# A hybrid streaming encoder layer on one core: the borders between recurrence, attention, merge and projections rearranged

## What is computed

```python
h = rmsnorm(x, norm_mix_g)
qkv, z, b_raw, a_raw, dq, dk, dv, gate_a, gate_b = split(h @ w_in)
o_a = gated_delta_rule(...)                    # branch A: 8 heads, chunks of 64 frames
o_a = rmsnorm(o_a, norm_g) * silu(z)
s = q k^T * 64 ** -0.5 - slope * dist          # branch B: two maps for each of 8 heads
p = softmax(s)
o_b = rmsnorm((p[0] - lam * p[1]) @ v) * (1 - lam_init)
x = x + (sigmoid(gate_a) * (o_a @ w_branch_a) + sigmoid(gate_b) * (o_b @ w_branch_b)) @ w_out
x = x + cross_attend(rmsnorm(x), mem_k, mem_v, w_mq, w_mo)     # 4 heads, 256 memory tokens
x = x + peer(rmsnorm(x))                       # 128*128 one-neuron experts
return rmsnorm(x)
```

## Time and profile before

| | us |
|---|---|
| median of 3 runs | 5154.19 |
| lowest and highest | 5153.65 to 5163.55 |
| the profiled execution | 5151.6 |
| its span, first to last instruction | 5150.0 |
| TensorE busy in it | 4952.7 |
| VectorE busy | 3119.4 |
| ScalarE busy | 1607.4 |

### The profile page before, as it was taken

One profiled execution on the slowest core, in us unless ns is written; L12 is line 12 of the kernel. 1 busy time (PEld: TensorE's weight loads), 2 busy tenths in 40 slices (PEclk: granted clock), 3 DMA queues, 4 the chain that ended last, 5 costly groups with the idle time before them and its releaser, 6 DMA issues.

```text
span 5150.0 us, 83445 instructions
## 1 busy us (share of the span) xinstructions
PE 4952.7 (96%) x35997; PEld 4795.7 (93%) x35997; DVE 3119.4 (61%) x3919; ACT 1607.4 (31%) x1776; POOL 744.1 (14%) x606
## 2 busy tenths in 40 slices
PE   8999999998999999999989999999999999999998
PEld 6999988887888899998989999999999999999998
DVE  5355544444445433322279988887676477777777
ACT  4444422223334321213132234443222222222222
POOL 0100000000000000000000022323443122222221
PEclk9999999999999999999999999999999999999999
DMA  6422232222332432231232268888998789999985
GB/s 229 163 103 101 97 94 83 78 86 103 104 103 95 151 122 85 83 114 64 84 131 99 104 241 332 328 324 328 337 345 327 275 328 337 333 335 329 330 327 210
DMA packets 262923, 1010.01 MB, mean 196 GB/s; under 512 B 47744, under 2 KB 127744, under 8 KB 176640
## 3 DMA queue, kind: packets, MB, share of 16 engines
q1 hardware_dynamic: 177696, 547.93, 30.4%
q0 software_dynamic: 68832, 442.58, 22.5%
q10 hardware_dynamic: 16128, 15.60, 0.9%
HBM read 918.77 MB, written 87.24 MB: 195 GB/s over the span
## 4 chain that ended last, share of the span: by engine, by line
PE 75%; DVE 11%; DMA 7%; issue 3%; ACT 2%; DVEq 2%; ACTq 0%; POOL 0%; SPq 0%; POOLq 0%; PEldq 0%
PE psum L1300 20%; PE psum L1112 11%; PE psum L1222 11%; PE psum L918 10%; PE psum L890 7%; PE psum L1129 4%; DMA tmp<-in_u,eidx 2%; DMA arena<-in_u,tiu 2%; PE psum L866 2%; DVE e_lo L2066 2%; PE psum L1268 2%; PE psum L851 2%; DMA arena<-in_u,eidx 1%; DVE arena L2231 1%; DVE tmp L2231 1%
## 5 line engine op out<-in xcount | busy, mean ns | idle before, releaser
L2066 DVE TENSOR_TENSOR e_lo<-ring,e_hi 128x2048 fp32r<-128x2048 f32 x270 | 618.7, 2291 | 284.7 <-ACT e_hi L1551 271.0
L1551 ACT ACTIVATE e_hi<-ring 128x2048 fp32r<-128x2048 f32 x270 | 517.7, 1917 | 811.3 <-PE psum L1300 659.6
L1222 PE MATMUL psum<-h_hi,e_hi 128*128 128x384 f32 x2032 | 698.0, 343 | 34.8 <-DVE e_lo L2066 34.2
L1300 PE MATMUL psum<-c_hi,e_hi 128*128 128x384 f32 x2048 | 686.8, 335 | 13.6 <-DVE H L2311 9.2
L1222 PE MATMUL psum<-h_hi,e_lo 128*128 128x384 f32 x2048 | 690.5, 337 | 0.0
L1222 PE MATMUL psum<-h_lo,e_hi 128*128 128x384 f32 x2032 | 687.1, 338 | 0.0
L1300 PE MATMUL psum<-c_lo,e_hi 128*128 128x384 f32 x2048 | 685.4, 335 | 0.0
L1300 PE MATMUL psum<-c_hi,e_lo 128*128 128x384 f32 x2048 | 685.3, 335 | 0.0
L918 PE MATMUL psum<-p_hi,e_lo 128*128 128x272 f32 x1792 | 519.4, 290 | 0.0
L1222 PEld LDWEIGHTS psum<-h_hi,e_hi 128*128 128x128 f32 x2032 | 383.8, 189 | 42.2 <-issue 19.1
L1300 PEld LDWEIGHTS psum<-c_hi,e_hi 128*128 128x128 f32 x2048 | 385.3, 188 | 18.8 <-DVE e_lo L2066 9.4
(11 more groups left out here) (461 smaller groups left out, 10461.3 us busy)
## 6 DMA issues: line engine op xcount, KB each, us to landing
ring<-in_weights SPq DMA_DIRECT2D x200, 1024.0 KB, 4.8
ring<-in_uT SPq DMA_DIRECT2D x128, 1024.0 KB, 5.4
ring<-in_v SPq DMA_DIRECT2D x128, 1024.0 KB, 9.0
hid<-tmp POOLq DMA_DIRECT2D x128, 192.0 KB, 5.9
gates<-arena POOLq DMA_DIRECT2D x12, 2048.0 KB, 10.1
arena<-hid SPq DMA_DIRECT2D x32, 768.0 KB, 11.1
arena<-gates SPq DMA_DIRECT2D x32, 768.0 KB, 15.0
gate_in<-tmp ACTq DMA_DIRECT2D x64, 136.0 KB, 3.4
```

What stands on the lines that cost most here:

```text
L1222: mm = nc.tensor.matmul(psum[:, 2 + r % 2, 0:ND], w, h[:, c, 0:ND], start=(c == 0 and i == 0), stop=(c == KD - 1 and i == 2))
L1300: mm = nc.tensor.matmul(psum[:, d, 0:ND], w, c[p // 2][:, 2 * (p % 2) + r, :], start=(first and r == 0 and j == 0), stop=(last and r == 1 ...
L1551: nc.scalar.activation(hi_slot(n, reg), e_raw[n % R], ACT.Copy).then_inc(w_rounded, 1)
L2066: nc.vector.tensor_tensor(e_lo[n % R], e_raw[n % R], as_f32(hi_slot(n, reg)), ALU.subtract)\
```

## The change

- **A tile between recurrence and attention.** TensorE fills a whole tile (32 units) after the last chunk, before it waits for `d_o`; ScalarE serves its first half before its own wait and its second after it. A head has 112 units instead of 116, with "vt" 6 instead of 12, a[0] 18 instead of 14, "obs" 4 instead of 6, and three of aT[3]'s six units placed as "os" in front of step 4's waits.
- **Splits and norms in attention.** `splits_at` places a split after the last step that has at least 8 units left until the tile is wanted; `norm_slot` puts the norm of a head after the first step of the next head that has no split.
- **Rounds later.** A round that falls due in an "a" or "obs" stretch is put off until the copy of the transposed probabilities, or the square root, has been made (`round_later`).
- **Branch A ahead of the last norm.** ScalarE rounds OA in the last head (after step 4's exponentials, copies and squares), VectorE splits it before the last norm; OB's first seven heads are rounded before the last one is done. TensorE no longer waits for `done`. The split of the second merge tile comes after OB's.
- **M's first half earlier.** Heads 0 to 7 of M are rounded once branch A of the last merge tile is through (`oa_used`), and split before that tile's merge. The round and split of the second w_out tile move behind that.
- **Sums and waits one tile later.** The sums of X's squares come after the first w_mq tile, the root after all of X is rounded; the first projection starts before ScalarE has taken the small rows (`ba_free`).
- **Three pieces of the cross-attention's output** are rounded in the last head.
- GpSimd waits for the distances before it loads those of the decode rows, and for `x_tile` instead of `x_done`.

```diff
-ATT_FILL = {"vt": 12, "a": (14, 12, 14, 16, 17), "aT": (8, 4, 3, 6, 4), "obs": 6}
+ATT_FILL = {"vt": 6, "a": (18, 12, 14, 16, 17), "aT": (8, 4, 3, 3, 4), "os": 3, "obs": 4}
...
-GDN_UNITS, ATT_UNITS = F_CHUNK * F_TILE, 116
+GDN_UNITS, ATT_UNITS = F_CHUNK * F_TILE, 112
...
+P_DONE = [ATT_FILL["vt"] + sum(ATT_FILL["a"][0:q + 1]) + sum(ATT_FILL["aT"][0:q]) + (ATT_FILL["os"] if q == 4 else 0)
+          for q in range(QT)]
+SPLIT_UNITS = 8
+def splits_at(h, q):
+    at = ATT_UNITS * h + P_DONE[q]
+    after = ATT_UNITS * (h + 1) + P_DONE[0] if q == QT - 1 else ATT_UNITS * h + P_DONE[q + 1]
+    last = h == HEADS - 1 and q == QT - 1
+    return [k for k in range(2, N_FILL - F_GDN + 1)
+            if F_TILE * (k - 1) >= at + SPLIT_UNITS and (last or F_TILE * (k - 1) < after + SPLIT_UNITS)]
+def norm_slot(h):
+    return next(q for q in range(QT) if not splits_at(h + 1, q)) if h + 1 < HEADS else None
...
             pool.wait_ge(fill_full, 2 * (F_GDN + 1))
+            pool.wait_ge(at["dist_in"], 16)
             pool.dma_start(ndist_s[0:NS, :], t["ndist_s"]).then_inc(at["dist_in"], 16)
...
             mm.then_inc(ba_full, 1)
-            pe.wait_ge(ba_free, 1)
...
                 pe.wait_ge(qk_sq, i * 2 + 2)
+                pe.wait_ge(ba_free, 1)
...
+            u = fill(u, F_TILE)
             pe.wait_ge(s["d_o"], NCH + 1)
...
                     if q == 4:
+                        u = fill(u, ATT_FILL["os"])
                         wait_first(at["cache_in"], h * 32 + 32)
                         wait_first(at["obs"], h * 2 + 1)
...
-            pe.wait_ge(at["done"], HEADS)
...
+                    if d == KD - 1 and k0 == 0:
+                        mm.then_inc(oa_used, 1)
                 mm.then_inc(tile_done, 1)
-            pe.wait_ge(acc_free, freed(T_OUT + 1))
             for d in range(KD):
                 split_tile(T_OUT + d, m_hi, m_lo, S_M)
-            tile_sums(pe, "cross")
             for d in range(KD):
                 split_tile(T_MQ + d, h_hi, h_lo, S_H)
+                if d == 0:
+                    tile_sums(pe, "cross")
...
+            u = serve(u, F_HALF)
             act.wait_ge(s["d_o"], NCH + 1)
             act.wait_ge(outs, 48)
             round_w(T_FILL + F_GDN + 1)
+            u = serve(u, F_HALF)
...
-                    u = serve(u, ATT_FILL["a"][q])
+                    later = []
+                    u = serve(u, ATT_FILL["a"][q], later)
+                    if h == HEADS - 1 and q == 4:
+                        round_branch(oa_hi, OA, 0, 3)
...
+                    round_later(later)
                     u = serve(u, ATT_FILL["aT"][q])
...
-                u = serve(u, ATT_FILL["obs"])
+                u = serve(u, ATT_FILL["obs"], later)
+                if h == HEADS - 1:
+                    round_branch(oa_hi, OA, 6, HEADS)
                 act.wait_ge(at["oss"], h + 1)
                 nc.scalar.activation(ort, aux[0], ACT.Sqrt, bias=eps, scale=1.0 / DH).then_inc(at["rt"], 1)
+                round_later(later)
...
-            act.wait_ge(fill_full, 2 * N_FILL)
+            round_branch(ob_hi, OB, 0, HEADS - 1)
             act.wait_ge(at["done"], HEADS)
-            for k in range(HEADS):
-                round_src(oa_hi, OA, S_OAB, k)
-            for k in range(HEADS):
-                round_src(ob_hi, OB, S_OAB, k)
+            round_branch(ob_hi, OB, HEADS - 1, HEADS)
...
                 if k == 0:
+                    act.wait_ge(oa_used, 1)
+                if k == HEADS:
                     act.wait_ge(tile_done, done(T_OUT - 1))
+                    round_w(W_MERGE + KD + 1)
                 round_src(m_hi, M, S_M, k)
...
                 if k == 1:
                     tile_squares(act, "cross", KD - 1)
-                    tile_root(act, "cross")
+            tile_root(act, "cross")
...
+                else:
+                    for k in range(OC_EARLY):
+                        round_src(m_hi, OC, S_OC, k)
...
-            head_norm(HEADS - 1)
-            split_w(T_MERGE + 1)
...
-            dve.sem_inc(merged, 2)
             for k in range(HEADS):
                 split_src(oa_lo, OA, oa_hi, k, S_OAB)
+            head_norm(HEADS - 1)
+            dve.sem_inc(merged, 2)
             for k in range(HEADS):
                 split_src(ob_lo, OB, ob_hi, k, S_OAB + HEADS)
+            split_w(T_MERGE + 1)
             for d in range(KD):
+                if d == KD - 1:
+                    for k in range(HEADS):
+                        split_src(m_lo, M, m_hi, k, S_M)
```

More of the change, by code:

```diff
@@ L62 @@
             "a_vn": 4, "a_o": 3}
-ATT_FILL = {"vt": 12, "a": (14, 12, 14, 16, 17), "aT": (8, 4, 3, 6, 4), "obs": 6}
+ATT_FILL = {"vt": 6, "a": (18, 12, 14, 16, 17), "aT": (8, 4, 3, 3, 4), "os": 3, "obs": 4}
 F_CHUNK = 3
-GDN_UNITS, ATT_UNITS = F_CHUNK * F_TILE, 116
+GDN_UNITS, ATT_UNITS = F_CHUNK * F_TILE, 112
 assert sum(GDN_FILL[k] for k in ("c_qb", "c_kv", "d_gu", "d_a", "d_rr", "a_vn", "a_o")) \
     + sum(GDN_FILL["d_r"]) + 5 * GDN_FILL["a_x"] == GDN_UNITS
-assert ATT_FILL["vt"] + sum(ATT_FILL["a"]) + sum(ATT_FILL["aT"]) + ATT_FILL["obs"] == ATT_UNITS
-assert GDN_UNITS * (NCH + 1) + ATT_UNITS * HEADS == N_FILL * F_TILE
+assert ATT_FILL["vt"] + sum(ATT_FILL["a"]) + sum(ATT_FILL["aT"]) + ATT_FILL["os"] + ATT_FILL["obs"] == ATT_UNITS
+assert GDN_UNITS * (NCH + 1) + F_TILE + ATT_UNITS * HEADS == N_FILL * F_TILE
 N_WEIGHTS = T_PQ + 16
-UNITS_AT = [ATT_UNITS * h + ATT_FILL["vt"] + sum(ATT_FILL["a"][0:q]) + sum(ATT_FILL["aT"][0:q])
-            for h in range(HEADS) for q in range(QT)] + [ATT_UNITS * HEADS]
+P_DONE = [ATT_FILL["vt"] + sum(ATT_FILL["a"][0:q + 1]) + sum(ATT_FILL["aT"][0:q]) + (ATT_FILL["os"] if q == 4 else 0)
[9 more added lines that the diff above has]
+    return next(q for q in range(QT) if not splits_at(h + 1, q)) if h + 1 < HEADS else None
 W_MERGE = T_MERGE
@@ L767, in _ @@
                 values_of(h)
-            pool.wait_ge(x_done, 2)
+            pool.wait_ge(x_tile, 2 * KD)
             pool.dma_start(t["x_mid"], X).then_inc(x_moved, 16)
@@ L1444, in _, with serve @@
             first_rows(HEADS - 1, True)
-            def serve(u, units):
+            def serve(u, units, later=None):
                 for half in range(u // F_HALF, (u + units) // F_HALF):
@@ L1461, in serve, with round_later @@
                     if b == 1 and n != F_GDN - 1:
-                        round_w(T_FILL + n + 2)
+                        if later is None:
+                            round_w(T_FILL + n + 2)
+                        else:
+                            later.append(T_FILL + n + 2)
                 return u + units
+            def round_later(later):
+                while later:
+                    round_w(later.pop(0))
             def gdn_block(c, dyn, u):
@@ L1504, in _, with round_branch @@
             round_w(T_FILL + F_GDN + 1)
+            u = serve(u, F_HALF)
+            def round_branch(hi, src, first, end):
+                for k in range(first, end):
+                    round_src(hi, src, S_OAB, k)
             for h in range(HEADS):
@@ L1533, in _ @@
                         nc.scalar.activation(osq[:, 0:NP_], ob[:, 0:NP_], ACT.Square)
+                        u = serve(u, ATT_FILL["os"])
+                    if h == HEADS - 1 and q == 4:
+                        round_branch(oa_hi, OA, 3, 6)
                 act.wait_ge(at["o"], h * 5 + 5)
@@ L1608, in _ @@
             act.drain()
-            for k in range(KD):
+            for k in range(OC_EARLY, KD):
                 round_src(m_hi, OC, S_OC, k)
@@ L1924, in _ @@
                 gdn_block(c, slice(c * CH, (c + 1) * CH))
+            split_w(T_FILL + F_GDN + 1)
             dve.wait_ge(at["dist_in"], 16)
@@ L1935, in head_norm @@
                                                in1=ort, op0=ALU.mult, op1=ALU.mult).then_inc(at["done"], 1)
-            def split_tiles(h, q):
-                for k in range(1, N_FILL - F_GDN + 1):
-                    if UNITS_AT[QT * h + q] <= F_TILE * k - 12 < UNITS_AT[QT * h + q + 1]:
-                        split_w(T_FILL + F_GDN + k)
             def attention_head(h):
@@ L1975, in attention_head @@
                                                    op0=ALU.mult, op1=ALU.add).then_inc(at["a"], 1)
-                    if q == 0 and h:
+                    if h and q == norm_slot(h - 1):
                         head_norm(h - 1)
-                    split_tiles(h, q)
+                    for k in splits_at(h, q):
+                        split_w(T_FILL + F_GDN + k)
             for h in range(HEADS):
                 attention_head(h)
-            head_norm(HEADS - 1)
-            split_w(T_MERGE + 1)
             def split_src(lo, src, hi, k, n):
@@ L1988, in split_src @@
                     .then_inc(src_split, 1)
+            for k in range(HEADS):
+                split_src(oa_lo, OA, oa_hi, k, S_OAB)
+            head_norm(HEADS - 1)
             dve.sem_inc(merged, 2)
             for k in range(HEADS):
```

(12 more changed lines are left out.)

9 lines of the change are left out of this document (5 added, 4 removed).

## The result

| | before | after |
|---|---|---|
| median, us | 5155.72 (4 runs) | 5100.21 (4 runs) |
| lowest to highest | 5153.65 to 5163.55 | 5086.02 to 5103.28 |
| profiled execution | 5151.6 | 5086.02 (its span 5084.5) |

The ratio of the mean times is 0.9884 (95%: 0.9869 to 0.9899), 60 us less; the two medians lie 55.5 us apart. The forecast was 5100.

A forecast was written before the change was run, and what follows sets the result against it. TensorE's chain of waits, with half clock after most over 2 us, was taken as the bound. Border terms summed to 54.5 us saved: 5151.6 to 5097.1, plus 2.6 for the median, forecast 5100, range 5087 to 5120.

The forecast's parts named there:

- Recurrence to attention: Between recurrence and attention: a filling tile covers the 13.3 us wait for head 0's rows; 15.2 us saved, 12.4 without the clock.
- Attention: In attention: waits for splits, output copy and probabilities and their slow stretches mostly go; 18.7 us saved, bounds 0 to 31.
- (a): After heads 1, 3 and 5: a round delays the next head's value copies; wait 1.8 us, three times, 5.5 lost.
- (b): In attention: norms and rounds come slightly late at some 16 joints; 0.25 us each, 4.0 lost, between 0 and 21.
- (c): In attention: half of the three value-copy waits may bring a slow clock stretch; 2.6 us lost, 0 to 5.1.
- Attention to merge: Border into the merge: 13.6 us lost before, less new waits for branch B, second tile, gates and clock; 7.0 saved, 2 to 11.
- Rival D: At the merge: X and gates come so late that branch A's gain is handed back at tile 2; 5107, chance 0.07.
- w_out to w_mq: Ahead of w_mq: a loss, X's sums on the path 1.8 us and a longer slow stretch 1.3; -3.1, 0 to -4.
- w_mo: At w_mo: one rounding and one split happen before, 1.3 us, and the slow stretch goes, 1.7; 3.1 saved.
- Rival C: Covers hold: attention's small joints cost nothing, no slow clock, gates in time; 5089, chance 0.11.
- B: Attention's waits only move: small joints near their upper bound, slow stretches at all value-copy waits; gain 5, 5113, chance 0.14.
- E: Postponed rounds stand before exponentials or copies at nearly every tile boundary; attention loses 101 us, 5189, chance 0.08.

## Why the prediction was right, step by step

**First projection**, 5.6 against 5.9: wait and half stretch, as its own experiment shows; the 0.4 taken for the moved wait did not come.

**Recurrence to attention**, 15.2 against 16.0: under 0.9 us of waiting was left, 0.5, and full clock there; the experiment with the tile behind the rows gives the whole back. The clock's part (2.8) is not safe: where the rows came 1.5 to 2 us later it was lost, and what is left is about the prediction's 12.4 without it.

**Attention**, 18.7 against 26.9: right in what goes and in (a), three waits of 1.7 where 1.8 was worked out. The term that was mis-sized is (b), the small joints, 16 x 0.25 = 4.0: the trace after has no wait for probabilities, splits or the output's copy at all. One such joint, the norm of head 0 within head 1, on VectorE and TensorE:

```profile
1341.87 0.78 DVE L1980 SCALAR_TENSOR_TENSOR arena<-tmp,lamb 128x544 f32<-128x544 f32 x1
1342.58 0.74 DVE L1994 SCALAR_TENSOR_TENSOR H<-H,const,psum 128x512 f32<-128x512 f32 x1
...
1347.25 0.75 DVE L2013 SCALAR_TENSOR_TENSOR H<-H,tmp 128x512 f32<-128x512 f32 x1
...
1341.29 1.13 PE L1074 MATMUL psum<-H 64*128 64x512 f32 x4
...
1348.48 0.60 PE L1085 MATMUL psum<-const,H 128*128 128x128 f32 x4
```

The norm ends at 1342.65, the scores at 1342.42, so VectorE is some 0.2 us late (I had 0.3 to 1.0), and the probabilities are done at 1348.00, 0.48 before TensorE takes them. I had set a slack of 0.6 against a delay of up to 1.0; both ends were off to the same side. (c) was 2.6, and one slow stretch came of three possible: 1.7. With (a) 0.3 smaller that makes 5.2 of the 8.2; of the rest, 1.0 us is waiting before that the rows of the waits name apart from my three (0.9 of it for the copied probabilities), and about 2 us I can't place. A part may lie in the reading of a wait, which no run here tests: matmuls of filling start 0.13 us apart and last 0.29, so idle time that is counted from the end of the last one falls short of the time lost by up to 0.16, by estimate 2.7 for the 17 waits that are gone.

On the table load, the time line above has the root 0.02 us behind the load of 1.28, and the copy wait is 1.7. The Trainium skill, "ScalarE: Activation LUTs", section "What ACT_TABLE_LOAD costs", adds a drain of about 1.38 us to each switch; by that the wait would have been 3.1. The row decided rightly.

**Attention to merge**, 7.0 against 3.6. The 2.3 us for branch B's residue came out as worked out, 0.4 for the second tile did not come. The step that was mis-sized is the third tile: 3.9 where I took 2.3 from a range of 0.7 to 4.0. The working was right in its order (X, gates, sigmoid, round, split), but the weight load beside them cost more than the 3.3 that I had as its upper end: gates 18.7 us after the norm instead of 14.8, 3.9 later. The terms that I named for this chain also make 28.8, not 29.2; the trace has about the missing 0.4, for the split starts behind the merge's third step (ended 1669.42) and not behind the round (1669.01). And the clock, 1.6 taken, was two stretches of 3.41, its upper end of 3.4. With my own upper ends the sum is 3.5, so the lower bound of 2 had no terms behind it. Rival D, given 7 in 100 with all of the 7.0 lost, holds for the order of the norm: alone it is worth 0.5 here and 7.1 with the gates early. The 3.6 that remain are nearly the 2.9 by which OA's early rounds shorten the first tile's wait even with the norm first (11.3 to 8.4), and those 0.5. So the part that the prediction counted on, TensorE at work on branch A during the norm, brought next to nothing, and the gain is left to the early rounds, which it had only as a step on the way; that is by difference, as no run makes the rounds late again.

**Merge to w_out**, 8.0 against 8.0: no wait, full clock. Only the profiles say so: no experiment undoes M's early half.

**w_out to w_mq**, -3.1 against -2.7: the loss is there, and 1.8 of it is the sums, shown by putting them back. The clock part, 1.3 taken, was 1.0 (4.66 us of work at half clock, 2040.44 to 2045.10, against 2.64), but the reason given for it failed: the stretch is as long with the sums in front, and shorter in two kernels with the same wait.

**w_mo**, 3.1 (its terms make 3.0) against 1.65: its wait fell from 2.4 to 0.9 and its slow stretch went; a slow stretch of 6.83 us at the memory scores, in place of 3.41, took about 1.5 back. No experiment undoes this border either.

The sum, 54.5 against 59.3, is 4.8 short: attention 8.2 too low, merge 3.4 and w_mo 1.45 too high, the rest within 0.8. That the median agrees with the forecast to 0.2 us is partly luck: by its stages the change is worth 59, and four more runs of the same kernel had a median of 5093.09. Rival C (5089, the covers hold) is nearly right for attention and wrong for the merge; B and E did not come.

## What to carry to other kernels

When a wait is taken away, ask of every transfer that was issued behind its cause whether that wait had been hiding it: here a queue's order (a bulk reload ahead of the first small operands) was free until the compute became early, and then took back 6.6 of 7.1 us. Deferred work goes behind the last step that somebody waits for, not just behind the next one: a 1.9 us round in front of two copies of 0.6 and 0.25 us cost 6.9 us, three waits and one slow stretch. Read a change stage by stage: here the total scatters by 15 us, a stage of the same kernel by 0.3, an untouched stage of its variants by up to 3.

## What the runs showed of the hardware that I had not expected

A wait's length does not tell what the clock does. Behind three waits of 1.7 us in the changed kernel it fell once, in the kernel with the old splits behind all three of them and behind three of four of 1.8 us; behind one of 2.5 us ahead of w_mq it fell for 3.41 us in one kernel and not at all in another with the same wait; behind 5.2 us there it was low for 6.83 us in most kernels, for 3.41 in two. So a short wait's price lies between itself and itself plus 1.7 us, and where it lies is not given by its length.

A weight load of 1 MB that ran beside X's 4.25 MB and the gates took 9.6 us (1656.10 to 1665.75); before, the two such loads between 1690 and 1730 took 4.8 (median), and the gates behind X, which had no load beside them, came 3.9 us sooner. So both transfers got slower. The Trainium skill, "DMA: Bandwidth & Descriptors", section "Queues, rings and completion order", says that each DMA engine takes packets from its queues in turn. The trace agrees: between 1656 and 1666 us 347 packets of X's queue and 144 of the weights' ran side by side.
